# Hybrid mLSTM / RG-LRU block on one core: the first three weight groups reordered, first loads in halves

## The reference

```python
n1 = rmsnorm(x, norm_mix_g)
q, k, v, o_pre, if_pre, x_r, g_r = split(n1 @ w_in)
# group A: 4 mLSTM heads of 256; logf = log_sigmoid(f_pre), b = cumsum(logf), running-max stabiliser,
#          weights exp(b_t - b_s + i_s - m_t) on causal q.k, times v; per-head RMSNorm; sigmoid(o_pre) gate
# group B: causal depthwise conv of x_r, two block-diagonal gates, h_t = a_t h_{t-1} + u_t, times gelu(g_r)
x = x + concat(A, B) @ w_out
gate, up = split(rmsnorm(x, norm_ffn_g) @ w_up)
x = x + (silu(causal_dwconv(gate)) * up) @ w_down
return rmsnorm(x, norm_final_g)
```

## Time and profile before

| | us |
|---|---|
| median of 3 runs | 1146.89 |
| lowest, highest | 1146.67, 1147.82 |
| the profiled execution | 1147.8 |
| its span, first to last instruction | 1145.9 |
| TensorE busy, share of the span | 1126.4, 98% |
| VectorE busy | 750.3, 65% |
| ScalarE busy | 581.8, 51% |

### The profile page before, as it was taken

The page is one execution under the profiler, slowest core; times in us unless marked ns, Lnnn a source line. Parts: engine busy times, 40 slices in busy tenths (PEclk is TensorE's granted clock), DMA queues, the critical chain, the costliest instruction groups (busy, mean ns, idle before and its releaser), DMA issues.

```text
span 1145.9 us, 18106 instructions
## 1 busy us (share of the span) xinstructions
PE 1126.4 (98%) x6018; PEld 968.7 (85%) x6018; DVE 750.3 (65%) x988; ACT 581.8 (51%) x769; POOL 51.8 (5%) x48
## 2 busy tenths in 40 slices
PE   8899999999999999999999999999999999999997
PEld 7688888888888888888888888888888888888885
DVE  5659567595685677666666766666666755556554
ACT  6547456474565664435444444444444554555454
POOL 0010000100000000000000000000000000002000
PEclk9899999999999999999999999999999999999998
DMA  7565747657555556665665666566566556555653
GB/s 242 163 203 151 209 128 222 172 145 213 183 199 195 181 160 196 201 189 167 208 192 165 207 194 184 170 212 188 163 214 192 197 189 196 191 192 187 197 189 109
DMA packets 166185, 213.56 MB, mean 186 GB/s; under 512 B 6764, under 2 KB 148332, under 8 KB 166032
## 3 DMA queue, kind: packets, MB, share of 16 engines
q1 hardware_dynamic: 165312, 210.79, 59.6%
q0 software_dynamic: 560, 2.24, 0.5%
q10 hardware_dynamic: 288, 0.21, 0.1%
HBM read 211.10 MB, written 2.11 MB: 186 GB/s over the span
## 4 chain that ended last, share of the span: by engine, by line
PE 94%; DVE 4%; ACT 1%; DMA 1%; issue 1%; SPq 0%; DVEq 0%; ACTq 0%
PE ps L1011 40%; PE ps L1125 27%; PE ps L1013 20%; PE ps L1007 3%; PE ps L1009 1%; DVE w L572 1%; DMA xres<-x_dram 1%; PE ps L985 1%; PE ps L1096 0%; DVE aT L578 0%; PE ps L1048 0%; PE ps L1078 0%; PE ps L1068 0%; ACT w L330 0%; ACT xn L330 0%
## 5 line engine op out<-in xcount | busy, mean ns | idle before, releaser
L1011 PE MATMUL ps<-xT,w 128*128 128x512 f32 x2048 | 717.5, 396 | 1.2 <-DVE w L572 0.7
L572 DVE TENSOR_TENSOR w<-raw,w 128x1024 fp32r<-128x1024 f32 x392 | 480.4, 1238 | 344.1 <-ACT w L330 343.5
L330 ACT ACTIVATE w<-raw 128x1024 fp32r<-128x1024 f32 x392 | 410.0, 1058 | 417.8 <-PE ps L1013 245.9
L1013 PE MATMUL ps<-xT,w 128*128 128x256 f32 x2048 | 569.7, 278 | 0.0
L1011 PEld LDWEIGHTS ps<-xT,w 128*128 128x128 f32 x2048 | 384.8, 188 | 91.1 <-DVE w L572 1.0
L1013 PEld LDWEIGHTS ps<-xT,w 128*128 128x128 f32 x2048 | 385.8, 188 | 0.3
L1125 PE MATMUL ps<-w,aT 128*128 128x512 f32 x1440 | 327.9, 389 | 0.9 <-DVE aT L578 0.9
L1125 PEld LDWEIGHTS ps<-w,aT 128*128 128x128 f32 x1440 | 269.8, 188 | 57.7 <-DVE aT L578 1.7
L330 ACT ACTIVATE fs<-fc 128x512 f32<-128x512 f32 x22 | 13.9, 634 | 101.1 <-DVE fc L906 101.1
L969 POOL TENSOR_TENSOR fs<-fs,rB 128x512 f32<-128x512 f32 x22 | 28.6, 1299 | 569.4 <-ACT fs L330 569.4
L1007 PE MATMUL ps<-w,xT 128*128 128x512 f32 x128 | 46.7, 408 | 2.6 <-DVE w L572 2.6
...
## 6 DMA issues: line engine op xcount, KB each, us to landing
raw<-w_up_dram SPq DMA_DIRECT2D x176, 512.0 KB, 4.6
raw<-w_in_dram SPq DMA_DIRECT2D x96, 512.0 KB, 3.8
raw<-w_down_dram SPq DMA_DIRECT2D x88, 512.0 KB, 4.2
raw<-w_out_dram SPq DMA_DIRECT2D x32, 512.0 KB, 4.8
xres<-x_dram SPq DMA_DIRECT2D x4, 512.0 KB, 8.1
y_dram<-xn SPq DMA_DIRECT2D x8, 256.0 KB, 3.0
bc<-rows POOLq DMA_DIRECT2D x4, 256.0 KB, 5.4
...
```

The lines of the kernel that those rows point to most:

```text
L330: return sc.activation(out_, in_, fn, **kw)
L572: v.tensor_tensor(w[:, s, :, 1, :], raw[:, s, :].rearrange("p (c n) -> p c n", c=CH), w[:, s, :, 0, :], ALU.subtract).then_inc(lo_ready, 1)
L1011: mm(full, w[:, s, c, 0, cut], xT[:, kt, :, :].rearrange("p a n -> p (a n)"), start=kt == 0, stop=False)
L1013: ins = mm(rest, w[:, s, c, 1, cut], xT[:, kt, 0, :], start=False, stop=kt == KT - 1)
```

## The change

- **Loads.** x chunk 0 comes as two DMAs of 256 columns with a semaphore each, weight unit 0 as two DMAs of two tiles. The 16 gain columns of `par` come first in ScalarE's queue, then the identity, then the rest of `par`.
- **First unit.** ScalarE, VectorE and TensorE treat unit 0 in two halves. TensorE transposes chunk 0, issues 6 more matmuls of ones (`KEEP_WARM`), multiplies the first half, transposes chunk 1, then multiplies the second half; for that the loop of `unit` over its tiles became a function of its own, `part_of_unit`.
- **Squares.** The pieces are 512 and 1536 columns for row block 0 and 512, 768 and 768 for row block 1; the first pieces come before bank 2's high part.
- **Row scales.** `spread_rows` moves from the middle of group 1 to right behind the gate products.
- **Gate chain.** On VectorE the chain from `gate_mid` to `f_abs` follows the row scales, and the splits of group 1's last two units and of group 2 are put between its steps; masks come after `f_abs`, the RG-LRU columns after the splits of group 2, q's addition before the split of unit (2,1). On ScalarE the two exp steps stand together and the two ln steps together, and the roundings are spread accordingly. The `gdif` transposes move from behind group 1 to before its last unit.

```diff
-WARM_UP = 8
+X_PIECES = [[(0, BANK), (BANK, D)], [(0, BANK), (BANK, BANK + 768), (BANK + 768, D)]]
+WARM_UP, KEEP_WARM = 8, 6
...
-                cols = slice(c * BANK, (c + 1) * BANK)
-                sp.dma_start(xres[:, :, cols], x_rows[:, :, cols]).then_inc(x_landed[c], 16)
+                first, last = c * BANK, (c + 1) * BANK
+                if c == 0:
+                    sp.dma_start(xres[:, :, 0:COLS], x_rows[:, :, 0:COLS]).then_inc(x_first_landed, 16)
+                    first = COLS
+                sp.dma_start(xres[:, :, first:last], x_rows[:, :, first:last]).then_inc(x_landed[c], 16)
...
-            load_group(0, in_v, COL_Q, load_x)
+            load_x(0)
+            sp.wait_ge(lo_ready, 1)
+            for c, landed in ((0, w_first_landed), (CH // 2, raw_landed[0])):
+                sp.dma_start(raw[:, 0, c * COLS:c * COLS + BANK].rearrange("p (c n) -> p c n", c=CH // 2),
+                             in_v[0, :, c:c + CH // 2, COL_Q:COL_Q + COLS]).then_inc(landed, 16)
+            for s in range(1, RING):
+                load_x(s)
+                load(0, s, in_v[s, :, :, COL_Q:COL_Q + COLS], raw[:, s, :].rearrange("p (c n) -> p c n", c=CH))
...
+            act_e.dma_start(par[:, PAR_GMIX:PAR_GMIX + KT], par_in[:, PAR_GMIX:PAR_GMIX + KT]).then_inc(gain_landed, 16)
             act_e.dma_start(ident, const_in[:, C_ID:C_ID + P]).then_inc(ident_landed, 16)
-            act_e.dma_start(par[:], par_in).then_inc(par_landed, 16)
+            act_e.dma_start(par[:, PAR_GMIX + KT:], par_in[:, PAR_GMIX + KT:]).then_inc(par_landed, 16)
             after(act_e, V0, "start")
             warm_sqrt(A0)
-            act_e.wait_ge(par_landed, 16)
-            for s in range(RING):
-                for b in (2 * s, 2 * s + 1):
-                    transposed_hi(A0, E0, PAR_GMIX, b)
-                round_units(0, [s])
-                if s == 2:
-                    act_e.wait_ge(gate_landed, 16)
-                    after(act_e, V0, "gw_zero")
-                    did(act_fn(gws[:, :, 0:2, 0:H], gw[:]), A0, "gw_hi")
+            act_e.wait_ge(gain_landed, 16)
+            transposed_hi(A0, E0, PAR_GMIX, 0)
+            act_e.wait_ge(w_first_landed, 16)
+            act_e.wait_ge(unit_used, 1)
+            act_fn(w[:, 0, 0:CH // 2, 0, :], raw[:, 0, 0:BANK].rearrange("p (c n) -> p c n", c=CH // 2)).then_inc(first_hi_ready, 1)
+            transposed_hi(A0, E0, PAR_GMIX, 1)
+            act_e.wait_ge(raw_landed[0], 16)
+            act_fn(w[:, 0, CH // 2:, 0, :], raw[:, 0, BANK:].rearrange("p (c n) -> p c n", c=CH // 2)).then_inc(hi_ready, 1)
             for r in range(ROWS):
                 squares(A0, r, 0)
-            round_units(1, range(2))
-            for r, n in ((0, 1), (1, 1), (1, 2)):
-                squares(A0, r, n)
+            transposed_hi(A0, E0, PAR_GMIX, 2)
+            round_units(0, [1])
+            for b in (3, 4, 5):
+                transposed_hi(A0, E0, PAR_GMIX, b)
+            round_units(0, [2])
+            act_e.wait_ge(gate_landed, 16)
+            after(act_e, V0, "gw_zero")
+            did(act_fn(gws[:, :, 0:2, 0:H], gw[:]), A0, "gw_hi")
+            round_units(0, [3])
+            for b in (6, 7):
+                transposed_hi(A0, E0, PAR_GMIX, b)
+            squares(A0, 0, 1)
+            round_units(1, [0])
+            for n in (1, 2):
+                squares(A0, 1, n)
             for r in range(ROWS):
                 std(A0, V0, r)
-            round_units(1, range(2, RING))
-            copy_half(0, 0, qT[:])
+            round_units(1, [1])
             after(act_e, E0, "gates")
             did(act_fn(grow[:], ps[0:64, B_SC, 0:S]), A0, "gate_half")
+            copy_half(0, 0, qT[:])
+            round_units(1, [2])
 
             after(act_e, V0, "lam_abs")
             did(act_fn(lp[:, 2, :], lp[:, 2, :], ACT.Exp), A0, "lam_exp")
-            after(act_e, A0, "lam_exp")
-            did(act_fn(lp[:, 2, :], lp[:, 2, :], ACT.Ln, bias=1.0), A0, "lam_ln")
             after(act_e, V0, "f_abs")
             did(act_fn(gtmp[F_ROW:F_ROW + H], gtmp[F_ROW:F_ROW + H], ACT.Exp), A0, "f_exp")
             after(act_e, A0, "f_exp")
             did(act_fn(gtmp[F_ROW:F_ROW + H], gtmp[F_ROW:F_ROW + H], ACT.Ln, bias=1.0), A0, "f_ln")
-            round_units(2, range(3))
+            after(act_e, A0, "lam_exp")
+            did(act_fn(lp[:, 2, :], lp[:, 2, :], ACT.Ln, bias=1.0), A0, "lam_ln")
+            round_units(1, [3])
+            round_units(2, range(2))
             after(act_e, V0, "neg_clip")
             did(act_fn(neg[:, 1, :], neg[:, 1, :], ACT.Exp), A0, "floor")
-            round_units(2, range(3, RING))
+            round_units(2, range(2, RING))
             copy_half(1, 1, kT[:])
...
-            dve.wait_ge(par_landed, 16)
-            for s in range(RING):
-                for b in (2 * s, 2 * s + 1):
-                    transposed_lo(A0, V0, PAR_GMIX, b)
-                split_units(0, [s])
-                if s == 2:
-                    after(dve, A0, "gw_hi")
-                    did(v.tensor_tensor(gws[:, :, 2:4, 0:H], gw[:], gws[:, :, 0:2, 0:H], ALU.subtract), V0, "gw_lo")
-            norm_base(A0, V0)
-            split_units(1, range(2))
-            norm_base1(A0, V0)
-            dve.wait_ge(ident_landed, 16)
-            diagonals(A0, V0)
-            split_units(1, range(2, RING))
-            add_half(0, 0, qT[:])
-            row_scales(V0, E0)
-            did(v.tensor_scalar(rmask[:, 0:S], rB[:, 0, :], small[:, RSTD:RSTD + 1], None, ALU.mult), V0, "rm0")
-            did(v.tensor_scalar(rmask[:, S:S + P], rB[:, 0, P:S], small[:, RSTD + 1:RSTD + 2], None, ALU.mult), V0, "rm1")
-            dve.wait_ge(tri_landed, 16)
-            for n, col in enumerate((0, S)):
-                after(dve, V0, f"rm{n}")
-                did(v.tensor_tensor(rmask[:, col:col + P], rmask[:, col:col + P], tri, ALU.mult), V0, f"tri{n}")
+            dve.wait_ge(gain_landed, 16)
+            transposed_lo(A0, V0, PAR_GMIX, 0)
+            dve.wait_ge(first_hi_ready, 1)
+            v.tensor_tensor(w[:, 0, 0:CH // 2, 1, :], raw[:, 0, 0:BANK].rearrange("p (c n) -> p c n", c=CH // 2),
+                            w[:, 0, 0:CH // 2, 0, :], ALU.subtract).then_inc(first_lo_ready, 1)
+            transposed_lo(A0, V0, PAR_GMIX, 1)
+            dve.wait_ge(hi_ready, 1)
+            v.tensor_tensor(w[:, 0, CH // 2:, 1, :], raw[:, 0, BANK:].rearrange("p (c n) -> p c n", c=CH // 2),
+                            w[:, 0, CH // 2:, 0, :], ALU.subtract).then_inc(lo_ready, 1)
+            transposed_lo(A0, V0, PAR_GMIX, 2)
+            split_units(0, [1])
+            transposed_lo(A0, V0, PAR_GMIX, 3)
 
             lru_par = par[:, PAR_LRU:PAR_LRU + LBLK * LRU_PAR].rearrange("p (b n) -> p n b", n=LRU_PAR)
             lam = lru_par[:, 7, :]
+            dve.wait_ge(par_landed, 16)
             did(v.tensor_scalar(lp[:, 3, :], lam, -1.0, None, ALU.mult), V0, "lam_neg")
             after(dve, V0, "lam_neg")
             did(v.tensor_tensor(lp[:, 2, :], lp[:, 3, :], lam, ALU.min), V0, "lam_abs")
             after(dve, V0, "lam_abs")
             did(v.tensor_scalar(lp[:, 3, :], lp[:, 3, :], 0.0, None, ALU.max), V0, "lam_relu")
+            did(v.tensor_scalar(lp[:, 0:2, :], lru_par[:, 5:7, :], 0.5, None, ALU.mult), V0, "half_bias")
+            did(v.tensor_scalar(hg[:], par[:, PAR_HEAD:PAR_HEAD + 2 * H], 0.5, None, ALU.mult), V0, "hg")
+
+            for b in (4, 5):
+                transposed_lo(A0, V0, PAR_GMIX, b)
+            split_units(0, [2])
+            after(dve, A0, "gw_hi")
+            did(v.tensor_tensor(gws[:, :, 2:4, 0:H], gw[:], gws[:, :, 0:2, 0:H], ALU.subtract), V0, "gw_lo")
+            split_units(0, [3])
+            for b in (6, 7):
+                transposed_lo(A0, V0, PAR_GMIX, b)
+            norm_base(A0, V0)
+            split_units(1, [0])
+            norm_base1(A0, V0)
+            dve.wait_ge(ident_landed, 16)
+            diagonals(A0, V0)
+            split_units(1, [1])
+            row_scales(V0, E0)
...
+            split_units(1, [2])
             after(dve, A0, "f_ln")
...
             did(v.tensor_tensor(gdif[:], grow[0:H], fsum[:], ALU.subtract), V0, "gdif")
+            split_units(1, [3])
             after(dve, V0, "gdif")
             did(v.tensor_tensor_scan(logf[:], one_row, gdif[:], 0.0, ALU.mult, ALU.max), V0, "cmax")
+            split_units(2, [0])
             after(dve, V0, "cmax")
             did(v.tensor_scalar(neg[:, 0, :], logf[:], -1.0, None, ALU.mult), V0, "neg_M")
             after(dve, V0, "neg_M")
             did(v.tensor_tensor(neg[:, 1, :], neg[:, 0, :], fsum[:], ALU.subtract), V0, "neg_m")
             after(dve, V0, "neg_m")
             did(v.tensor_scalar(neg[:, 1, :], neg[:, 1, :], FLOOR_LN, None, ALU.min), V0, "neg_clip")
-            split_units(2)
+            add_half(0, 0, qT[:])
+            split_units(2, range(1, RING))
+            after(dve, A0, "lam_ln")
+            after(dve, V0, "lam_relu")
```

(25 more changed lines are left out.)

45 lines of the change are left out of this document (25 added, 20 removed).

## The result

| | before | after |
|---|---|---|
| median of 4 runs each, us | 1147.16 | 1138.31 |
| lowest, highest | 1146.67, 1147.82 | 1137.79, 1139.0 |
| the profiled execution, its span | 1147.8, 1145.9 | 1137.79, 1136.0 |

The account below looks back on a forecast made before the run. TensorE, busy 98%, bounds the kernel; time is gained only where it waits or runs at its lower clock. Group 2 starting 7.35 us earlier plus 1.75 of clock gives 9.1 off median 1146.89: 1137.8, range 1136.3 to 1141.0.

Parts of the forecast that it names:

- the hole ahead of group 2: TensorE's idle stretch between groups 1 and 2: it goes, group 2 starting at 40.2 instead of 47.54, 7.35 us earlier.
- First product 8.9: Kernel start: first half weight unit ready at 8.9 instead of 10.76, so the first product comes 1.86 us earlier.
- The halves do overlap: Start loads: the fixed DMA part of about 2 us overlaps between halves; paid in turn, the start would gain nothing.
- Fillers and clock: Before the first product: 6 extra matmuls end at 8.3, hide behind the 8.9 and fill TensorE's idle stretch.
- Rival A: Start: the clock does not hold, fillers or pairs run slow, about 2.1 us later; result 1139.9, chance 0.15.
- The wait of unit 2: First units: TensorE, ready at 17.75, waits 0.85 us for VectorE's split, ready at 18.5.
- Gate chain: VectorE from 28.7 to 40.15: reordered steps and splits keep up with TensorE, which starts group 2 at 40.2.
- rival B: VectorE from 28.7 to 40.15: steps 1.5 us longer in all delay group 2; 1139.3 to 1141.0, chance 0.12.
- The clock of 1.75: First 6 pairs of group 2: without the hole they avoid the lower clock, saving 1.75 us.
- C: Early units: TensorE's waits at 13.5 and 17.75 vanish because steps run shorter; 1136.4, chance 0.06.
- D: Ahead of group 2: the hole moves instead of going, only the start counts; 1145.2, chance 0.03.
- E: Head 0's decay on VectorE waits for broadcast rows, delaying group 4's splits; slower than before, chance 0.02.

Follow-up runs that it names:

- no_fillers: Changed kernel without the 6 filler matmuls (KEEP_WARM = 0): 1139.71 us, ratio 0.9933 to the kernel before.
- changed_again: The changed kernel run again unaltered in a later job: 1138.33 us, ratio 0.9919 to the kernel before.
- start_only: Changed kernel with gate chain, row scales and splits back in the old order, new start kept: 1145.09 us, ratio 0.998 to the kernel before.
- scales_late: Changed kernel with only the row-scale matmuls moved back to the middle of group 1: 1144.08 us, ratio 0.9974 to the kernel before.
- dve_delay: Changed kernel with one extra VectorE memset (1.34 us) ahead of logf: 1139.74 us, ratio 0.9927 to the kernel before.
- three_fillers: Changed kernel with 3 filler matmuls instead of 6: 1138.00 us, ratio 0.9916 to the kernel before.
- raw_whole: Changed kernel with weight unit 0 loaded in one DMA, still rounded, split and multiplied in halves: 1138.06 us, ratio 0.9913 to the kernel before.
- x_whole: Changed kernel with x chunk 0 loaded in one DMA again: 1139.38 us, ratio 0.9927 to the kernel before.
- weight_second: Changed kernel with the first weight half issued before the second x half: 1137.71 us, ratio 0.9909 to the kernel before.
- fill_between: Changed kernel with first weight half issued before second x half, and fillers between the first two banks' transposes: 1137.85 us, ratio 0.9914 to the kernel before.
- scales_early: Kernel before with only the row-scale matmuls moved right behind the gate products: 1143.81 us, ratio 0.9967 to the kernel before.

## Why the prediction was right

It was right in mechanism and size: the hole ahead of group 2 and the slow pairs behind it went, as summed (7.78 and 1.70 us against 7.35 and 1.75). One of its steps hit its number because errors cancelled, one held by luck, and one term was mis-sized.

- **First product 8.9, measured 8.87, by cancelling errors.** ScalarE began at 5.66, not 6.4. The half split was taken to be ready at 8.9 because VectorE was; in fact ScalarE waited for the weight half, which landed at 7.4, and VectorE's split waited for ScalarE: the weight's chain set it, not that over x. The split ended at 8.76, and so did the fillers, forecast for 8.3: they started at 7.26, since the second half of x landed only at 6.76. The identity, too, came later than the 4 that was taken: 3.6 us after its issue at 1.23, just ahead of the first transposes at 4.90. ScalarE, then VectorE, after:

```profile
5.66 0.84 ACT L344 ACTIVATE xT<-ps,par 128x256 fp32r<-128x256 f32 x2 [1.97 <-PE ps L1032]
7.41 0.63 ACT L344 ACTIVATE w<-raw 128x512 fp32r<-128x512 f32 x1 [0.91 <-DMA raw<-w_in_dram]
```

```profile
8.07 0.69 DVE L669 TENSOR_TENSOR w<-raw,w 128x512 fp32r<-128x512 f32 x1 [0.58 <-ACT w L344]
```

- **The halves do overlap, but bring little.** Issued at 0.76 and 1.26 the halves of x landed at 4.1 and 6.76; the whole had landed at 5.56 before. So the first half came 1.5 us earlier and the second 1.2 later, 2.7 us behind the first, and it cost nothing only because the weight half was later still. The Trainium skill, page "DMA: Bandwidth & Descriptors", section "Anatomy of one DMA", has about 2 us of fixed cost for a DMA, measured on GpSimd's path, while these loads are issued by SyncE. The 2.7 us of this profile would fit such a part paid in turn plus the time for the data, but in the seven other profiles with the same order of these loads (changed_again, start_only, scales_late, dve_delay, no_fillers, three_fillers, raw_whole) the halves landed 1.2 to 2.1 us apart, which would not. So overlap, as the prediction had it, is the better reading, and the late second half here is a spread of the landings.
- **Fillers and clock: partly luck.** That the filled stretch keeps the clock is shown by no_fillers. That the fillers would be short (8.3) was argued from the transposes at 9.11 of the kernel before, but when the passes become fast differs from execution to execution. Rival A took 0.23 a pass to be a risk; of the nine profiles with 6 fillers two show just that (x_whole and weight_second, first products at 10.1) and one in part (fill_between, 1.94 us). Its price of 2.1 us is near the 1.8 between executions of weight_second, and its chance of 0.15 was not too high. In both profiles of the changed kernel the passes were fast.
- **The wait of unit 2: 0.85 forecast, 0.41 measured.** This is the mis-sized term. The profile's idle times (0.43 and 0.16) count from the modelled end of the transposes, 1.04 us after their start; but where a product follows at once it starts 0.79 after them (10.35 and 11.14), which is the 0.8 of the forecast. Counted so, the first wait is 0.68 (12.62 to 14.09) against 0.55, and unit 1 starts at 14.09 against 14.05: right. The second is 0.41 (17.03 to 18.23) against 0.85. I had put VectorE's five parameter steps at 0.2 us each; they took 0.65 us in all (14.74 to 15.39), so the split was ready at about 18.1 instead of 18.5. Hence the gate products end at 27.64, not 28.05, and group 2 starts at 39.76, not 40.2.
- **Gate chain.** Forecast: copy at 28.7, split (1,2) ready at 32.8, `gdif` at 35.45, split (1,3) at 36.6, q's addition at 40.15. Measured: 28.29, 32.4, 35.0, 36.07, 39.55. All are 0.4 to 0.6 early, about as much as the gate products, so the steps between them were right. dve_delay showed that the chain is on the path; rival B failed only because no step was longer than taken.
- **No drain at the table load.** The Trainium skill's page "ScalarE: Activation LUTs", section "What ACT_TABLE_LOAD costs", adds a drain of 1.38 us to each switch of tables; by the prediction's estimate it would have given 41.5 for group 2. ScalarE's rows after show the load at 31.69 for 1.28, at once behind the exp step and with the next step at once behind it. The trace agrees with the page on the load and shows no drain:

```profile
31.25 0.42 ACT L344 ACTIVATE gtmp<-gtmp 4x256 f32<-4x256 f32 x1
31.69 1.28 ACT L344 ACT_TABLE_LOAD   x1
32.98 0.42 ACT L344 ACTIVATE gtmp<-gtmp 4x256 f32<-4x256 f32 x1
```

- **The clock of 1.75: 1.70 measured.** It is gained because the hole went; scales_early, where a hole of 1.96 was left, still paid it. The rival's 1143.5 for that kernel was nearer (1143.81) than my 1141.7: the clock fell behind the shorter hole too.
- **Rivals C, D, E.** C's waits shrank but did not vanish. D did not occur: no hole is left. E did not either: `arg0` starts at 53.52 without a wait for the broadcast rows.
